# Two transformer blocks on one core: a new order of the work between the MLP's end and the first expert gathers

## The reference

```python
m = jnp.square(jax.nn.relu(h @ mlp_w1[l])) @ mlp_w2[l]
x = x + rms_norm(m, post_mlp_g[l])
...
h = jnp.concatenate([meta, x], axis=1)
for layer in range(DEPTH_2):
    hn = rmsnorm(h, norm_mix[layer])
    mix = pool_mixer(hn, pool_w[layer], pool_scale[layer])      # layer 0; layer 1 is attention
    h = h + mix
    h = h + peer(rmsnorm(h, norm_ffn[layer]), peer_wq[layer], peer_keys[layer], peer_u[layer], peer_v[layer])
```

## Time and profile before

| what | value |
|---|---|
| median of 3 runs | 1828.96 us (1827.97 to 1830.66) |
| the profiled execution, its own time | 1828.82 us |
| its span, first to last instruction | 1827.0 us |
| mean granted TensorE clock | 0.833 of full speed |
| busy share PE / DVE / ACT / POOL | 75% / 64% / 33% / 30% |
| moved by DMA | 681.19 MB, mean 373 GB/s |
| chain that ended last | DMA 38%, PE 28%, DVE 12%, ACT 5% |

### The profile page before, as it was taken

How to read it: one execution, slowest core, us unless ns; L and a number is a source line. 1 busy time by engine, 2 the same in 40 slices (tenths; PEclk the granted TensorE clock), 3 DMA queues, 4 the chain that set the end, 5 groups by cost and what they waited for, 6 DMA issues and landing times.

```text
span 1827.0 us, 19983 instructions
## 1 busy us (share of the span) xinstructions
PE 1377.8 (75%) x6240; PEld 549.8 (30%) x6240; DVE 1170.0 (64%) x2705; ACT 611.0 (33%) x1545; POOL 551.1 (30%) x633
## 2 busy tenths in 40 slices
PE   9999999978874645698677865785787765655566
PEld 7856666654431000122122221221232210101011
DVE  5831334168776777756786647767877577677764
ACT  2421011124342324433444323443543333333332
POOL 2001232013432333322433224322343334333331
PEclk9999999999996667799877887897897967676667
DMA  9048697559999999999999999999999999999997
GB/s 358 6 175 346 203 369 268 230 201 408 420 420 419 420 419 419 421 417 413 420 394 418 412 419 397 419 417 416 388 411 418 420 421 421 421 421 416 418 420 291
DMA packets 118187, 681.19 MB, mean 373 GB/s; under 512 B 11789, under 2 KB 13969, under 8 KB 50113
## 3 DMA queue, kind: packets, MB, share of 16 engines
q0 software_dynamic: 78336, 553.68, 73.5%
q1 hardware_dynamic: 39745, 126.23, 18.0%
HBM read 678.30 MB, written 1.05 MB: 372 GB/s over the span
## 4 chain that ended last, share of the span: by engine, by line
DMA 38%; PE 28%; DVE 12%; ACT 5%; issue 4%; DVEq 3%; POOL 2%; ACTq 1%; another core or an unknown queue 0%; POOLq 0%
DMA big<-in_peer_uv,expert 35%; PE ps L669 7%; DVE big L682 6%; PE ps L1909 6%; PE ps L1898 6%; PE ps L833 5%; DMA normed<-in_peer_uv,expert 3%; POOL big L635 2%; DVEq L529 2%; ACT placed L713 1%; ACT L713 1%; ACT L690 1%; ACT placed L717 1%; DVE residual L729 1%; PE ps L645 1%
## 5 line engine op out<-in xcount | busy, mean ns | idle before, releaser
L669 PE MATMUL ps<-big,placed 128*32 128x512 f32 x1992 | 603.3, 801 | 379.0 <-ACT placed L717 371.5
L682 DVE CUSTOM_DVE_ANT_0 big<-big,ps 128x1024 f32<-128x1024 f32 x498 | 595.7, 1219 | 338.7 <-DMA big<-in_peer_uv,expert 317.7
L635 POOL DMA_INDIRECT big<-in_peer_uv,expert x498 | 474.1, 952 | 1011.6 <-PE ps L669 838.1
L713 ACT ACTIVATE placed<-sel,dots 128x32 f32<-128x32 f32 x512 | 163.4, 319 | 777.1 <-DVE dots L682 750.3
L669 PEld LDWEIGHTS ps<-big,placed 128*32 128x32 f32 x1992 | 82.3, 122 | 814.5 <-ACT placed L717 710.1
L833 PE MATMUL ps<-big 128*128 128x512 f32 x384 | 193.2, 641 | 1.9 <-DVE big L1138 1.4
L717 ACT ACTIVATE placed<-placed,gate 128x32 f32<-128x32 f32 x512 | 164.6, 321 | 35.4 <-issue 0.3
L1909 PE MATMUL ps<-big,sc 128*128 128x512 f32 x256 | 115.5, 595 | 0.0
L1898 PE MATMUL ps<-ua,big 128*128 128x256 f32 (+1 forms) x512 | 110.6, 371 | 2.9 <-PEq L75 2.9
L833 PEld LDWEIGHTS ps<-big 128*128 128x128 f32 x384 | 72.1, 202 | 119.1 <-issue 112.7
L1898 PEld LDWEIGHTS ps<-ua,big 128*128 128x128 f32 x512 | 94.3, 195 | 27.8 <-issue 17.7
(11 more groups left out here) (372 smaller groups left out, 1273.5 us busy)
## 6 DMA issues: line engine op xcount, KB each, us to landing
big<-in_mlp_w SPq DMA_DIRECT2D x16, 2048.0 KB, 15.9
big<-in_peer_wq SPq DMA_DIRECT2D x2, 8192.0 KB, 26.8
big<-in_w_kv SPq DMA_DIRECT2D x32, 512.0 KB
big<-in_peer_wq SPq DMA_DIRECT2D x32, 512.0 KB
big<-in_w_in SPq DMA_DIRECT2D x5, 2048.0 KB, 17.8
big<-in_peer_uv,expert POOLq DMA_INDIRECT x530, 12.6
big<-in_w_q SPq DMA_DIRECT2D x16, 512.0 KB
big<-in_w_o SPq DMA_DIRECT2D x16, 512.0 KB
```

Source lines behind the costliest of these rows:

```text
L635: nc.gpsimd.indirect_dma_start(out=pair_row(n), out_offset=None, in_=rows, in_offset=bass.IndirectOffsetOnAxis(ap=expert[:, n // TOPK % DE ...
L669: last = nc.tensor.matmul(acc[r:r + TOK, :], placed[:, n % RING, :], pair_row(n)[:, D + BANK * half:D + BANK * (half + 1)], start=(opens a ...
L682: nc.vector.tensor_tensor_reduce(out=row, in0=row, in1=rows_x, scale=1.0, scalar=0.0, op0=ALU.mult, op1=ALU.add, accum_out=dots[:, u % 2, ...
L713: a.activation(to, sel32[:], ACT.Gelu, scale=dots[:, u % 2, k:k + 1])
```

## The change

- **MLP's end.** Step 31 of tile 1 is split: its second bank's part is put behind tile 0's pool sums. The gain is multiplied straight out of PSUM (`gained`), before the root mean is known; `added` then scales and adds in one operation, for tile 0 in two halves. ACT takes the squares of tile 0 by halves (`half_squares`).
- **Pool stage, tile 0.** The bands are scaled by the tile's reciprocal instead of the rows (`band0`), and PE reads `h` itself.
- **Unit 0's queries.** `head_transposes` transposes the 32 raw rows of unit 0 from `h`, in two lots of four small transposes; the copy out multiplies by the norm's gain by channel (a new vector row, `G_FFN0`). Queries of unit 0 use these columns. The reciprocal root mean is spread over the partitions by a matmul of one column, and ACT applies it as the scale of the query copy (`head_scale`).
- **Order.** On PE, behind unit 0's scores: the row product, tile 0's transposes, unit 1's queries to scores, and then all of tile 1's pool stage (sums and products). On DVE, behind `first_experts`: the copies of tile 0's transposes, tile 1's pool norm, stages 0 to 2 of unit 0, tile 1's pooled copies, stage 3. `add_mixed` of tile 1 is put behind step (0, 0), `ffn0_norm` of tile 1 behind step (0, 1), the copies of its transposes behind steps (0, 2) and (0, 3); on PE its transposes stand in `late_queries_pe` 2 and 3, on ACT its squares behind slot 3's weight. `zero_products` are gone from this part.
- **Gathers.** Gather 0 is issued from the best key of each half alone, gathers 1 to 7 from the 8 best as before. The place in `hn` is now n % 8 = 6; the place over the pool weights is n % 8 = 7 and waits for tile 1's products (`mixed` 4).
- **Loads.** The gain row `ffn0_row` is loaded at the start of the MLP stage, into `four_times`; the keys are loaded as soon as the MLP's gain rows are used.

```diff
-            dve_inverse_rms(dve, t, P, t, "ffn0")
+            dve.wait_ge(S("ffn0_std"), t + 1)
+            step(dve, nc.vector.reciprocal(stats[:, 9 + t:10 + t], stats[:, 6 + t:7 + t]), "ffn0_scale")
...
+        def head_transposes(pe, j):
+            pe.wait_ge(S("h1"), j + 1)
+            for c in range(4):
+                k = 4 * j + c
+                last = nc.tensor.transpose(bank(j)[:, TOK * c:TOK * (c + 1)], h[0:TOK, 0, P * k:P * (k + 1)],
+                                           ident[0:TOK, 0:TOK])
+            last.then_inc(S("head_t"), 1)
...
 def queries_pe(pe, u):
+            elif u == 3:
+                pe.wait_ge(S("h1"), 4)
...
+                if u == 0 and k == 6:
+                    pe.wait_ge(S("ffn0_scale"), 1)
+                    nc.tensor.matmul(bank(5)[:, 0:1], select[:], stats[:, 9:10], start=True, stop=True)\
+                        .then_inc(S("scale_spread"), 1)
+                cols_k = head_cols[:, k, :] if u == 0 else hnt[:, k, at:at + TOK]
...
 def peer_head_pe(pe, other_tile):
             scores0_pe(pe, 0)
-            other_tile()
-            queries_pe(pe, 1)
-            pe.wait_ge(S("h1"), 4)
+            pe.wait_ge(S("ffn0_normed"), 1)
+            pe.wait_ge(S("gain1_used"), 2 * NT)
...
+            for j in range(2):
+                ffn0_transposes(pe, 0, j, j)
+            queries_pe(pe, 1)
             query_columns_pe(pe, 1)
             scores0_pe(pe, 1)
-            ffn0_transposes(pe, 1)
+            pe.wait_ge(S("ffn0_scores_out"), 2)
+            other_tile()
...
 def late_queries_pe(pe, x):
-            if x == 0:
-                pe.wait_ge(S("ffn0_t_out"), 4)
+            if x in (2, 3):
+                pe.wait_ge(S("ffn0_normed"), 2)
+                if x == 3:
+                    pe.wait_ge(S("ffn0_t_out"), 3)
+                ffn0_transposes(pe, 1, x - 2, 1)
...
 def first_experts(dve):
+            v.tensor_scalar(expert[:, 0, 0:1], half_i[:, 1, 0:1], half_f[:, 0, 0:1], None, ALU.add)\
+                .then_inc(S("first_experts_ready"), 1)
...
 def peer_gpsimd(pool):
-                if n == 0:
-                    pool.wait_ge(S("first_experts_ready"), 2)
+                if n < 2:
+                    pool.wait_ge(S("first_experts_ready"), n + 2)
...
                 if n == 2:
+                    pool.wait_ge(S("mixed"), 2)
+                if n == 4:
+                    pool.wait_ge(S("mlp_done"), NT)
+                if n == MOVING:
+                    pool.wait_ge(S("pool_w_scaled"), 2)
+                if n == RING - 1:
                     pool.wait_ge(S("mixed"), 2 * NT)
-                if n == 6:
-                    pool.wait_ge(S("ffn0_normed"), 2)
-                if n == RING - 1:
-                    pool.wait_ge(S("ffn0_t"), 4)
...
 def peer_vector(dve, other_norm, other_pooled, other_added):
             first_experts(dve)
-            other_tile()
+            for j in range(2):
+                ffn0_transposes_out(dve, 0, j, j)
+            other_norm()
             scores_ready(dve, 0)
-            route(dve, 0, 0)
-            route(dve, 0, 1)
-            ffn0_norm(dve, 1)
-            route(dve, 0, 2)
-            ffn0_transposes_out(dve, 1)
+            for stage in range(3):
+                route(dve, 0, stage)
+            other_pooled()
             route(dve, 0, 3)
...
+                    if (s, j) == (0, 0):
+                        other_added()
+                    if (s, j) == (0, 1):
+                        ffn0_norm(dve, 1)
+                    if s == 0 and j >= 2:
+                        ffn0_transposes_out(dve, 1, j - 2, 1)
...
-                for q in range(STEPS_MLP - HELD, STEPS_MLP):
-                    last = down(q, (1,))
-                last.then_inc(S("mlp_done"), 1)
...
-                zero_products(pe, AWAKE)
-                pe.wait_ge(S("pool_normed"), 2)
-                pool_sums(0)
-                pe.wait_ge(S("pool_w_scaled"), 2)
-                pool_products(0)
-                pe.wait_ge(S("pool_normed"), 3)
-                pool_sums(1)
-                zero_products(pe, 7)
-                ffn0_transposes(pe, 0)
-                zero_products(pe, 3)
-                peer_head_pe(pe, lambda: pool_products(1))
+                down(STEPS_MLP - 1, (1,), (0,))
+                pool_sums(0)
+                down(STEPS_MLP - 1, (1,), (1,)).then_inc(S("mlp_done"), 1)
+                pe.wait_ge(S("pool_w_scaled"), 2)
+                pool_products(0, (0, 1, 2))
+                head_transposes(pe, 0)
+                pool_products(0, (3,))
+                head_transposes(pe, 1)
+                peer_head_pe(pe, other_tile)
```

## The result

The changed kernel takes 1834.74 us (median of 9 runs, 1832.88 to 1835.97); the kernel before beside it takes 1830.2 (9 runs). The ratio is 1.0026, 95% interval 1.0016 to 1.0037: **slower**, by 4.8 us of 1829 (3 to 7). I had forecast no change, 1829.3, with 0.67 for it and 0.14 for slower. The pair of profiled executions lies 6.3 us apart (spans 1827.0 and 1833.3).

A forecast was written before the change was run, and what follows sets the result against it. The time was taken as the gather stream's effective start plus a constant. Gains in the head were paid back until gather 16 set that start at 393.3 against 392.9, +0.4 us, so 1829.3 us; range 1823.3 to 1833.

The forecast's parts named there:

- What bounds: Whole kernel: time is the moment from which the gather stream no longer runs dry, plus a constant.
- the effective start: Time at which an unbroken gather stream would have had to begin: 392.9 us before, 393.3 predicted.
- The head: Stretch up to the first gather: first maximum 5.6 us sooner, gather 0 8.5 us sooner, at 380.5.
- PE's idle stretch and first clock fall: PE empty from 381.4 to 384.75, then unit 1's queries at the lower clock: 1.4 us extra, ending 389.85.
- Only then* tile 1's sums, 3.5: 395.8: PE behind unit 1's scores: tile 1's pool sums take 3.5 us from 392.25; first dot product at 399.6.
- Gather 7: Gather waiting on POOL for tile 1's products, done at 399.5: issued at 399.8.
- The step that decides: PE's wait on tile 1's norm (422.4), with queries up to unit 4's ahead of slot 8's value: done at 429.0.
- Gather 16: Gather waiting for slot 8's value: issued at 430.8 against 429.65, moving the effective start by +0.4 us.
- (c): Tile 1's stage behind unit 1 costs more: dots no sooner than 403, gather 16 at 434.2, 1832.7 us; chance 0.08.
- (b): PE's clock falls in the head: unit 0's queries take 7.3 us, all behind 3.7 later, 1833.0 us; chance 0.07.
- (a): Lead kept: gather 16 before 424.8, gather 8 binds, 5.6 us less, 1823.3 us; chance 0.19 including partly kept leads.
- without both clock drops: Bound without PE's two priced clock drops: 1.4 and 1.1 us less, gather 16 at 428.3, 1827.2 us.

The follow-up runs named there:

- warm_and_late: Changed kernel with zero products on PE around unit 1's queries and scores, and tile 1's transposes with their norm wait behind the step's queries; 1830.39 us, ratio 1.0001.
- warm: Changed kernel with zero products, read by nobody, in the three places where PE idles; 1832.48 us, ratio 1.0010.
- exp_early: Changed kernel with late tile 1 transposes, tile 1's sums before unit 1's queries, unit 0's exp earlier on ScalarE, 14 zero products; 1823.09 us, ratio 0.9960.
- late_transposes: Changed kernel with tile 1's transposes and their norm wait moved on PE behind the queries in steps (0, 2) and (0, 3); 1830.07 us, ratio 1.0004.
- norm_wait: exp_early with tile 1's transposes and norm wait put back ahead of unit 2's scores and unit 4's queries; 1828.33 us, ratio 0.9993.

## Why the prediction was wrong, point by point

- **What bounds** was right: the effective start, worked out from the rates, gives the span of all thirteen kernels within 2 us.
- **The head** was right to 0.2 us at its end. Predicted and measured: gather 0 380.5 and 380.43, gather 1 383.6 and 383.43. The pool sums start at 363.28 (363.4) and the first maximum comes at 378.20 (378.35). In between two errors cancel: the queries of unit 0 start at 371.43, 0.7 us sooner than predicted (372.1), and take 0.5 us longer to the first maximum. That part is luck.
- **PE's idle stretch and first clock fall** were right in place (the clock is at 0.50 from 384.5 to 388). Unit 1's queries took 384.59 to 391.34, 6.75 us and not 5.1, and ScalarE's copy of them came at 391.96 instead of 389.85, 2.1 us late. The clock alone does not account for it: with the full clock throughout this stretch, this copy came at 391.85 (warm_and_late) and 392.05 (warm). In the changed kernel PE has 24 matmuls from 388 to 389 us, then 17, 3 and 1 in the next three windows of 1 us, and the profile shows nothing that the gaps between them wait for. In exp_early, with the full clock, the 64 matmuls of unit 1's queries take 5.9 us from 388.4 and those of unit 2's 3.7 us from 399.1. What held PE up in 389 to 392 is open. So the price that I had put on this fall did not show, and a delay that was not in my sum did.
- **The step that failed is "*Only then* tile 1's sums, 3.5: 395.8".** The sums began at 394.5 (predicted 392.25) and the copy behind them at 401.33: 6.8 us. I had read 3.5 from a stretch at full clock, where it is 3.64 (371.37 to 375.01). Behind unit 1's queries, PE had 2.40 us of work in 390 to 395, and the clock fell a second time at 394.8. It stayed low through the sums and the first 3.9 us of the products, to 405.0. I priced two falls, after idle stretches, and not this one, after a stretch of short waits on ScalarE. The pair warm and warm_and_late (one execution of each) shows its price in the same code: 6.9 and 3.8 us from the sums' start to the copy behind them, 4.2 us on D0. Of D0's error (404.7 for 399.6, 5.1 us) the late start of the sums is 2.2 (the open delay above) and the sums 3.3 (3.0 of them the clock, by the 3.8 of warm_and_late); a shorter tail takes 0.4 back.
- **Gather 7** came at 407.0, not 399.8: the products began 5.3 us late, behind the sums, and took 5.6 us and not 3.7. The stream moved next to nothing from 401 to 408. I had foreseen a thin stretch from 402 to 405 ahead of gather 8, not this. It cost nothing at the end, because gather 16 permits a later start (436.75 + 2.5 - 40 = 399.3) than gather 7 (407.02 + 2.5 - 17.5 = 392.0).
- **The step that decides** was right: the wait on the norm with unit 4's queries behind it. From the norm's end (427.9) to gather 16 it took 8.8 us, predicted 8.4, and PE had been idle for 4.8 us before, predicted 5. late_transposes takes about 4 us off the changed kernel, norm_wait puts 4.2 on the fast one.
- **Gather 16** at 436.75 and not 430.8: 5.1 from D0, 0.4 from the stretch D0 to slot 8's dot product (23.2 us, predicted 22.8), 0.4 behind the norm. The effective start moved by 5.9 and not 0.4. So what made the kernel slower than the one before has two parts: the wait on the norm, which the sum had, and the late dots, which it had not.
- **Rivals.** (c), with 0.08, is what happened: tile 1's stage behind unit 1 cost more, dots after 403; gather 16 came 2.5 us later than even (c) has it (434.2). Its chance was too low, because my bounds let the clock only be better than assumed in that stretch, never worse. (b), a fall in the head, did not come: 1.00 from 375 to 380, and no fall before 384. The Trainium skill, TensorE: Matmul & The Clock Gate, section Part 4: PE-mode transpose, says that a transpose does not count as PE-busy in the way a product does. This trace does not show a fall by it: the clock is 1.00 through the eight small transposes at 368.71 and 371.07 (0.43 us for each four), which lie between products, with no zero products behind 360 us. (a), the lead kept, is real but needs another order: exp_early.
- **Small slips in the sum.** Stages 0 to 2 without the norm are 6.2 us in the rows and not 6.0, and without both clock drops the sum gives 1826.9, not 1827.2. Neither changes the outcome.

What stays open: what holds unit 1's queries up for some 2 us, why the clock falls in one execution of the same code and not in another, and how much of the changed kernel's 4.8 us it makes on average, as the timed runs show no clock for the stretch. The changed kernel with nothing but a full clock was not obtained.

## What to carry to other kernels

When a stream through a ring bounds the kernel, write down for each ring turn the start that its gather permits, and change the largest; to move only the first one moves a lead into a later hole. When work is reordered on one in-order engine, follow what stands behind every wait on all the others: one wait in front of 6 us of ready work cost 4 us here, and one exp behind two copies hid 5 to 6 us of gain (ratio 0.9994 against 0.9969 and 0.9960). Price matmuls behind a stretch of waits at both clock levels, and prefer an order in which another engine is busy meanwhile to padding with zero products: here the order without padding had 0.9969, the padded old order 0.9998.

## What the runs showed of the hardware

- The granted clock stayed at its lower level (0.50) from 394.8 to 405.0 us while PE was listed busy 5.00 of 5 us in both windows, on the sums' and products' matmuls. In the kernel before, where it fell at 395.5 with PE idle, it was back at 402.3, behind 2.8 us of score products and transposes from 399.5.
- The same code lost the clock at 391.8 in one execution and kept it in another, with PE busy 5.2 and 4.9 us of the 7 before; D0 differs by 4.2 us.
- Two table loads around a square root between Gelus cost 1.28 us each and nothing besides: what stands behind each starts 0.01 to 0.02 us after its end, and the second load starts 0.02 us after the square root's end. These are ScalarE's rows of the changed kernel's timeline:

```profile
415.96 1.28 ACT L242 ACT_TABLE_LOAD   x1
417.25 0.29 ACT L242 ACTIVATE stats<-stats,eps 128x1 f32<-128x1 f32 x1
417.56 1.28 ACT L769 ACT_TABLE_LOAD   x1
418.86 0.32 ACT L769 ACTIVATE placed<-sel,dots 128x32 f32<-128x32 f32 x1
```

Slot 4's weight begins at 418.86, 2.9 us behind its dot product's end, and gather 12 did not bind.
